# Routing's one-hots trade engines: plain ones in one VectorE comparison, gated ones token by token on GpSimd

## The reference, cut to what matters

```python
s1, i1 = lax.top_k(s[:, :, 0], K)
s2, i2 = lax.top_k(s[:, :, 1], K)
cand = (s1[..., :, None] + s2[..., None, :]).reshape(T, H, K * K)
sc, ci = lax.top_k(cand, K)
e1 = jnp.take_along_axis(i1, ci // K, axis=-1)
e2 = jnp.take_along_axis(i2, ci % K, axis=-1)
idx = e1 * PEER_NKEYS + e2
g = jax.nn.softmax(sc, axis=-1)
...
a = jnp.einsum('cd,chkd->chk', xc, u[ic])
act = (jax.nn.gelu(a.astype(jnp.float32)) * gc).astype(xc.dtype)
return jnp.einsum('chk,chkd->cd', act, v[ic])
```

## Time and profile before

| what | us |
|---|---|
| median of 3 runs | 4061.15 (4058.92 to 4061.73) |
| span of the profiled execution | 4058.1 |
| TensorE busy | 3871.2 (95%) |
| VectorE busy | 2202.3 (54%) |
| ScalarE busy | 1481.4 (37%) |
| GpSimd busy | 526.9 (13%) |

### The profile page before, as it was taken

One profiled execution on the slowest core, in us unless ns is written; L12 is line 12 of the kernel. 1 busy time (PEld: TensorE's weight loads), 2 busy tenths in 40 slices (PEclk: granted clock), 3 DMA queues, 4 the chain that ended last, 5 costly groups with the idle time before them and its releaser, 6 DMA issues.

```text
span 4058.1 us, 49083 instructions
## 1 busy us (share of the span) xinstructions
PE 3871.2 (95%) x20360; PEld 3097.5 (76%) x20360; DVE 2202.3 (54%) x3887; ACT 1481.4 (37%) x1877; POOL 526.9 (13%) x748
## 2 busy tenths in 40 slices
PE   7998999999899899999899999999999999999999
PEld 6754788888765678877777877877888888888887
DVE  3283643333647454464553457878944666654444
ACT  3255431222244632225553433444544222222222
POOL 0000000000000000000002100676773111100000
PEclk9998999999999999999999999999999999999999
DMA  6300123233120122232114223345546565643332
GB/s 246 138 1 1 73 73 125 104 125 115 42 75 1 42 83 94 95 123 74 55 44 155 89 98 125 135 156 157 176 156 228 189 194 184 191 135 114 114 125 83
DMA packets 109839, 459.85 MB, mean 113 GB/s; under 512 B 9216, under 2 KB 43120, under 8 KB 68912
## 3 DMA queue, kind: packets, MB, share of 16 engines
q1 hardware_dynamic: 82048, 354.96, 24.4%
q0 software_dynamic: 27568, 101.74, 8.4%
HBM read 389.04 MB, written 67.63 MB: 113 GB/s over the span
## 4 chain that ended last, share of the span: by engine, by line
PE 49%; DVE 2%; ACT 2%; POOL 1%; DMA 1%; issue 1%; DVEq 0%; ACTq 0%; POOLq 0%
PE ps L624 13%; PE ps L626 13%; PE ps L625 13%; PE ps L2761 2%; POOL OH L2897 1%; PE ps L2534 1%; PE ps L2307 1%; PE ps L2326 1%; PE ps L2548 1%; POOL Y L2897 0%; PE ps L1946 0%; PE ps L2083 0%; PE ps L1947 0%; PE ps L1948 0%; PE ps L2747 0%
## 5 line engine op out<-in xcount | busy, mean ns | idle before, releaser
L624 PE MATMUL ps<-HH,WH 128*128 128x512 f32 x2760 | 1058.7, 384 | 29.0 <-DVE HL L950 16.2
L625 PE MATMUL ps<-HL,WH 128*128 128x512 f32 x2760 | 1043.7, 378 | 0.0
L626 PE MATMUL ps<-HH,WL 128*128 128x512 f32 x2760 | 1040.8, 377 | 0.0
L495 DVE TENSOR_TENSOR WL<-stage,WH 128x2048 fp32r<-128x2048 f32 x239 | 548.1, 2293 | 443.9 <-ACT WH L485 442.9
L485 ACT ACTIVATE WH<-stage 128x2048 fp32r<-128x2048 f32 x239 | 455.8, 1907 | 526.3 <-PE ps L626 492.5
L624 PEld LDWEIGHTS ps<-HH,WH 128*128 128x128 f32 x2760 | 524.0, 190 | 141.9 <-issue 34.0
L626 PEld LDWEIGHTS ps<-HH,WL 128*128 128x128 f32 x2760 | 522.3, 189 | 104.1
L625 PEld LDWEIGHTS ps<-HL,WH 128*128 128x128 f32 x2760 | 523.8, 190 | 98.2 <-issue 1.2
L624 PE MATMUL ps<-AHp,WH 128*128 128x512 f32 x1024 | 405.1, 396 | 0.4 <-DVE ALp L3036 0.4
L626 PE MATMUL ps<-AHp,WL 128*128 128x512 f32 x1024 | 405.0, 395 | 0.0
L625 PE MATMUL ps<-ALp,WH 128*128 128x512 f32 x1024 | 405.0, 395 | 0.0
(11 more groups left out here) (436 smaller groups left out, 4928.8 us busy)
## 6 DMA issues: line engine op xcount, KB each, us to landing
stage<-in_w SPq DMA_DIRECT2D x64, 1024.0 KB, 4.8
stage<-in_u SPq DMA_DIRECT2D x64, 1024.0 KB, 4.8
stage<-in_v SPq DMA_DIRECT2D x64, 1024.0 KB, 4.8
stage<-in_w_mod SPq DMA_DIRECT2D x40, 1024.0 KB, 4.8
GR<-gdram POOLq DMA_DIRECT2D x32, 1024.0 KB, 8.1
AR<-adram POOLq DMA_DIRECT2D x88, 256.0 KB, 3.4
adram<-GR SPq DMA_DIRECT2D x21, 1024.0 KB, 4.1
gdram<-GST SPq DMA_DIRECT2D x16, 1024.0 KB, 5.6
```

Source lines behind the costliest of these rows:

```text
L495: dve.e.tensor_tensor(k.WL[o % 2][:, 0:w], k.stage[n % 2][:, 0:w], k.WH[o % 2][:, 0:w].bitcast(F32), ALU.subtract).then_inc(*dve.done("sla ...
L624: pe.e.matmul(o, wh[:, kk, cs], L.hh[:, kk, z], start=first, stop=False)
L625: pe.e.matmul(o, wh[:, kk, cs], L.hl[:, kk, z], start=False, stop=False)
L626: mm = pe.e.matmul(o, wl[:, kk, cs], L.hh[:, kk, z], start=False, stop=last)
```

## The change

VectorE's eight comparisons per piece, each with the multiplication by the gate, become one comparison without the gate over eight tokens: both operands are broadcast, IO over the tokens and E1 over the 128 columns. GpSimd's eight comparisons stay eight, and each now multiplies by the gate too. The product of the two one-hots is the same. No wait, buffer or position in the order changes. The lines of the new VectorE instruction are 2814 to 2817 of the changed kernel.

```diff
             oh = k.OH.take(dve, (tt, i), ("g_mm", (tt, i)))
             dve.wait_ge("chosen", tt)
             dve.wait_ge("iota", 0)
-            for t in range(8):
-                tok = 128 * tt + 8 * i + t
-                op = dve.e.tensor_scalar(oh[:, 0, t, :], k.IO[:, :], k.E1[:, tok:tok + 1], k.GG[:, tok:tok + 1],
-                                         ALU.is_equal, ALU.mult)
-            op.then_inc(*dve.done("hot1", (tt, i)))
+            tok = 128 * tt + 8 * i
+            dve.e.tensor_tensor(
+                oh[:, 0, :, :], k.IO[:, :].rearrange("p (o n) -> p o n", o=1).broadcast_to([128, 8, 128]),
+                k.E1[:, tok:tok + 8].rearrange("p (t o) -> p t o", o=1).broadcast_to([128, 8, 128]),
+                ALU.is_equal).then_inc(*dve.done("hot1", (tt, i)))
...
             for t in range(8):
                 tok = 128 * tt + 8 * i + t
-                op = pool.e.tensor_scalar(oh[:, 1, t, :], k.IO[:, :], k.E2[:, tok:tok + 1], None, ALU.is_equal)
+                op = pool.e.tensor_scalar(oh[:, 1, t, :], k.IO[:, :], k.E2[:, tok:tok + 1], k.GG[:, tok:tok + 1],
+                                          ALU.is_equal, ALU.mult)
             op.then_inc(*pool.done("hot2", (tt, i)))
```

## The result

The changed kernel takes 4118.89 us (median of 4 runs, 4116.2 to 4120.64) against 4061.44 for the kernel before (4 runs on the same chip): a ratio of 1.014, 95% interval 1.0128 to 1.0153. It is slower by 57 us. The forecast was 4070.5, the range 4060 to 4120. The sign is as forecast, the size is six times the sum (9.4 us). The result lies at the upper edge of the range, and not by the sum: the range had room for a rival, GpSimd as the bound, that had been given a chance of 0.22.

What follows compares the result with a forecast made beforehand. TensorE, busy 95%, was taken as the bound, losing time only where it waits. Tile ends 8.4 - 0.5 + 1.3 plus 0.2 in the middles gave +9.4 us on 4061.15: 4070.5, range 4060 to 4120.

Steps and rivals of the forecast that it cites:

- GpSimd as the bound: Rival, chance 0.22: GpSimd's second operation and scalar cost 0.2 to 0.58 us per instruction, giving 4087 to some 4198 us.
- the ends of the tiles: GpSimd's last three pieces delay TensorE: 4.2 us each at tiles 0 and 2, -0.5 at tile 1, +1.3 at tile 3.
- the middles: Between a tile's DMAs GpSimd's longer pieces were to fit, with only 0.2 us added for close meetings.
- Term 2: GpSimd's instruction gets a second operation and second scalar: 0.10 us each, 0.8 per piece, with 0 and 0.58 as bounds.
- slower clock: TensorE's clock was to cost nothing new, since its slower stretches follow waits that exist already.
- The limit of 7.9 us a piece: Middles: 27.7 us less copy, start, DMA and 0.14, over three GpSimd pieces, leaves 7.9 us per piece.
- The forecast's own 7.4: GpSimd's expected mean piece: 5.74 + 0.9 + 0.8 = 7.4 us, said to fit with 0.5 to spare.
- Term 1: VectorE's new two-input comparison, 1.21 us, blocks GpSimd: 0.9 us lost per comparison that meets it at work.
- the discount that the prediction made: GpSimd's loss beside a two-input VectorE instruction was put 0.17 us below that instruction's duration, at most 1.04 of 1.21.
- The 1.1 us that VectorE saves buy nothing: VectorE's saving per piece, 70 us in all, was to gain only 1.1 us at tile 1's end.
- faster by relief: Rival, chance 0.06: VectorE's long two-input instructions leave GpSimd's last pieces at tile 0's and 2's ends, 4051 to 4055 us.

Runs made afterwards that it cites:

- e3: Kernel before, with GpSimd's comparison also multiplying by the constant 1.0, no second scalar read from memory: 4063.96 us, ratio 1.0014.
- e1: Kernel before, with the gate multiplication moved to GpSimd; VectorE keeps eight token-by-token comparisons, now plain: 4087.83 us, ratio 1.0069.
- e2: Changed kernel with GpSimd's plain comparison of before, so the gates are left out and VectorE's one comparison stays: 4060.08 us, ratio 1.0001.
- e5: Kernel before, but from the fourth piece on VectorE makes only one of eight one-hots: 4053.68 us, ratio 0.9982.
- e4: Kernel before, with the plain one-hots of each tile's piece 14 made by VectorE in one comparison instead of by GpSimd: 4059.53 us, ratio 1.0001.
- e10: Kernel before, with both DMAs of GST issued from SyncE's queue, so GpSimd never waits for ScalarE's copy: 4059.55 us, ratio 0.9996.
- e7: e4 with the softmax's three VectorE instructions also moved behind the first pick: 4061.47 us, ratio 1.0008.
- e8: Kernel before, with only the softmax's three VectorE instructions moved behind the first pick: 4061.56 us, ratio 1.0008.
- e12: Kernel before, with both GST's DMAs on SyncE's queue and piece 14's plain one-hots on VectorE: 4061.86 us, ratio 1.0007.
- e14: e10 with the change made for pieces 14 and 15 alone, the exponential behind ScalarE's slab half, and the softmax as in e7: 4055.30 us, ratio 0.9992.
- e9: Changed kernel with each tile's piece 14 made by VectorE alone, gated one-hots token by token, plain ones in one comparison: 4085.35 us, ratio 1.0064.

## Why the prediction was right or wrong

**Where the time would be lost: right for the engine, wrong for the place.** TensorE's waits grew only for GpSimd, VectorE's relief made its two waits in the spread disappear, and the comparison takes what was computed. But the forecast put all but 0.2 us at the ends of the tiles, and two thirds of the new waits stand in the middles.

**Term 2, the first step that failed.** It was taken as 0.10 us per instruction; it is 0.194, of which 0.115 is the second operation and 0.079 the second scalar (e3). The prediction's case "GpSimd becomes the bound" is what came, and its figure for 0.2 us was 4087. The Trainium skill ("GPSIMD Engine Reference", section "3.1 Elementwise — side-by-side cycle accounting") would have the second operation free up to two per element; e3's 707 ns against 592 disagree, and the measurement decides.

**Its size, once more.** Even with 0.19 the prediction's sum would have been some 26 us, not 57. (In its case for 0.2 us tile 1 comes to 1.9 by its own terms, not 1.3.) The profiled executions differ by 61 us. 7 of these lie ahead of the spread, where the two programs are the same: GpSimd's first one-hot starts at 2541.7 before and at 2548.8 after. 54 lie in the spread:

| in the spread, us | forecast | measured |
|---|---|---|
| TensorE's waits at the ends of the tiles (last three pieces, choice) | +9.2 | 20.6 to 33.9, +13 |
| its waits in the middles | +0.2 | 0 to 25.9, +26 |
| slower clock | 0 | some +10 |
| not accounted for | | 5 |

The clock is the second term that was put at nothing. The mean granted clock is 0.978 over the 4119.3 us of the changed kernel's profiled execution, and was 0.982 over 4058.1. These means must not be put down to the change as a whole: by the clock records of the two traces TensorE was at the lower of its two levels (1.2 instead of 2.4 GHz) for 115 us before and 129 us after ahead of the spread, where nothing was changed, and for 28 us and 49 us in it. The 20 us more in the spread are worth some 10 us of TensorE's work. The products behind the longer waits show it, in 3.65 us at tile 0's end, where 1.78 is usual. No run had the waits without the slower clock, so this part is worked out and not tried apart.

**The middles: the third step that failed, and the largest.** The limit of 7.9 us a piece came from the kernel before, where GpSimd waits for ScalarE's copy ahead of every DMA. It leaves out the piece that GpSimd makes ahead of that DMA. Counted whole, GpSimd makes four pieces and one issue in the 29.5 us that TensorE takes for four pieces, so a piece may take (29.5 - 1.26) / 4 = 7.1 us; above that it falls behind, and can only use up the lead that it has over TensorE since the tile's start. The forecast's own 7.4 was above it already. In e1 the first 13 pieces of a tile take 7.5 us on average, and the lead still lasts (1.3 us of waits in the middles); in the changed kernel they take 8.25, and it does not. The changed kernel shows the loss: 33.0 us from DMA to DMA in tile 0 (2631.57 to 2664.56), 3.5 more than TensorE takes, with no wait for the copy at the second and third DMA of the tile.

**Why the halves are not additive.** In the spread GpSimd is either at work or waiting, so what is added to its work comes first out of its room, and only then out of the time. e2 adds 48 us of work, the room shrinks by 46, and nothing is lost. e1 adds 131, the room shrinks by 102, 28 are lost. The changed kernel adds 174, the room shrinks by 118, 57 are lost, and the 35 us of room that remain lie ahead of a tile's first DMA and at the turns of the tiles, outside the stretch in which it falls behind. In e1 the middles still hold: 36.7 of its 38.0 us of waits are at the ends. With the comparison's blocks on top they no longer do.

**Term 1, the block: the mechanism right, the size near.** Forecast 0.9 us per comparison that meets GpSimd. In e2's trace 28 slowed instructions of GpSimd had the comparison as the longest two-input instruction beside them, and lost 0.86 us each. By the piece it is 0.74 in e2, and on top of e1, whose own comparison is not without cost, 8.45 - 7.79 = 0.66. What the prediction did not think of: an instruction of GpSimd can be kept out across two of VectorE's that follow each other. One that began with piece 15's comparison (timeline):

```profile
2677.34 1.22 DVE L2814 TENSOR_TENSOR OH<-IO,TA 128x1024 f32<-128x1024 f32 x1
...
2677.50 3.84 POOL L2897 TENSOR_SCALAR OH<-IO,TA,TD 128x128 f32<-128x128 f32 x1
...
2678.48 2.28 DVE L2860 TENSOR_TENSOR Y<-RS,IO 128x2048 f32<-128x2048 f32 x1
```

It ends at 2681.34, 0.58 after L2860. The rule of the Trainium skill ("SBUF — State Buffer", section "SBUF: two separate sides"), that GpSimd is blocked fully while VectorE has the pair, agrees here: the instruction lost 3.05 us of the 3.26 that the two still lasted when it began. The 0.2 us less are the discount that the prediction made, and it held too.

**"The 1.1 us that VectorE saves buy nothing": wrong by a few us.** e5 has 2.0 us of relief per piece and gains 7 us. The forecast of the change stays the same, because the block takes it back (e2).

**The rival "faster by relief".** Its place was right in part: e4 and e10 show that, with GpSimd out of the way, VectorE's chain from the slab's half to the choice's result holds the ends with almost the same waits. Two engines hold them at once; relieving either gives nothing. Of the six runs that relieved one of them or moved a part of its chain in the kernel before (e4, e7, e8, e10, e12, e14), none moved the time by what can be told.

**Still open.** e1 loses 28 us where the prediction's sum, with 0.194 for term 2 and no block, gives some 12. In its trace the spread is 28 us longer than before; 17 of them are waits, and 47 us at the lower clock instead of 28 are worth some 9. Why its ends wait 16 us more is shown only in part: the last three pieces of a tile take 27 us on average instead of 21, where 24 x 0.19 makes 4.6 of the 6, and they begin later, since GpSimd has less room ahead of them.

## What to carry to other kernels

When work moves to an engine that is idle by the page, add up all that it does in one round of the bound engine, with its disturbed mean and not its undisturbed time, and compare: here four pieces and a DMA issue in 33.0 us against 29.5, in an engine that was 13% busy. A limit read from a chain with waits in it holds only as long as the waits are there. As long as the engine still waits, added work comes out of its waits and looks free, as in e2; so two changes that cost nothing or little alone can cost much together. Replacing eight one-input instructions by one two-input instruction halves VectorE's time and takes time from GpSimd, here 0.74 us for 1.1 saved, so count it on both. And before an end is given to one engine, look at the next one behind it: when two chains end close to each other, an edit to one gains no more than the distance to the other, here nothing that can be told.

## What the runs showed that I had not expected

A GpSimd comparison over 128 x 128 floats took 592 ns, with a multiplication by a constant 707, with a multiplication by a scalar from memory 786. Beside VectorE's plain comparison, with one scalar from memory, a GpSimd instruction of 0.78 us took 0.91 (e1); beside the comparison with the multiplication by a second scalar, one of 0.59 took 0.60 (the kernel before) and one of 0.79 took 0.82 (e9, seven of them). No run was made to try this by itself.

The disturbance by VectorE grows with GpSimd's own load: of the 367 us of one-hots before, 303 are 512 x 0.592, and 64 are disturbance. In e2 the 64 comparisons alone raise it to 112; in the changed kernel, with the same comparisons and longer instructions of GpSimd, it is 541 - 402 = 139.
